# A two-block layer stack on one core: eleven small edits to the written order of VectorE, ScalarE, GpSimd and TensorE

## What is computed

```python
def first_block(x, ...):
    for l in range(2):
        x = layer_norm(ALPHA * x + 0.5 * swiglu(x, ffn1_w13[l], ffn1_w2[l]), ...)
        x = layer_norm(ALPHA * x + mixer(x, w_in[l], ...), ...)      # hgrn2 recurrence + gated spatial unit
        x = layer_norm(ALPHA * x + 0.5 * swiglu(x, ffn2_w13[l], ffn2_w2[l]), ...)
def second_block(x, ...):
    for l in range(2):
        x = x + 0.5 * rms_norm(swiglu(rms_norm(x, g[0]), ...), g[1])
        x = x + rms_norm(token_mixer(rms_norm(x, g[2]), ...), g[3])  # dilated attention + two-way mLSTM
        x = x + 0.5 * rms_norm(swiglu(rms_norm(x, g[4]), ...), g[5])
```

## Time and profile before

| | before |
|---|---|
| device time, median of 3 | 2114.63 us |
| profiled execution: device time | 2114.63 us |
| profiled execution: span | 2112.9 us |
| TensorE matmul busy | 2090.4 us, 99% |
| VectorE busy | 1686.0 us, 80% |
| ScalarE busy | 1081.8 us, 51% |
| GpSimd busy | 84.5 us, 4% |
| mean rate of all DMA | 187 GB/s |
| granted TensorE clock | full in all 40 slices |

### The profile page before, as it was taken

How to read it: one execution, slowest core, us unless ns; L and a number is a source line. 1 busy time by engine, 2 the same in 40 slices (tenths; PEclk the granted TensorE clock), 3 DMA queues, 4 the chain that set the end, 5 groups by cost and what they waited for, 6 DMA issues and landing times.

```text
span 2112.9 us, 28855 instructions
## 1 busy us (share of the span) xinstructions
PE 2090.4 (99%) x10552; PEld 1774.3 (84%) x10552; DVE 1686.0 (80%) x3158; ACT 1081.8 (51%) x1568; POOL 84.5 (4%) x127
## 2 busy tenths in 40 slices
PE   8999999999999999999999999999999999999998
PEld 7887999888788799988878887988888888888886
DVE  6888766888888877778888887779888888678886
ACT  6445554544544455444454446575445445665543
POOL 0000010000000000000000001010000000101000
PEclk9999999999999999999999999999999999999999
DMA  7765755566566574656646666346665765645663
GB/s 249 234 194 169 224 166 157 188 217 191 174 218 196 174 234 139 190 168 224 196 153 213 215 191 196 125 136 207 214 195 171 220 196 163 185 140 165 214 191 98
DMA packets 314368, 395.56 MB, mean 187 GB/s; under 512 B 17972, under 2 KB 272212, under 8 KB 313972
## 3 DMA queue, kind: packets, MB, share of 16 engines
q1 hardware_dynamic: 309120, 375.52, 57.6%
q0 software_dynamic: 4944, 18.14, 2.7%
q10 hardware_dynamic: 164, 0.06, 0.0%
HBM read 392.59 MB, written 1.06 MB: 186 GB/s over the span
## 4 chain that ended last, share of the span: by engine, by line
PE 93%; DVE 4%; ACT 1%; issue 1%; DMA 1%; POOL 0%; SPq 0%; DVEq 0%; POOLq 0%; ACTq 0%
PE bank L309 25%; PE bank L311 25%; PE bank L310 25%; PE bank L303 4%; PE bank L304 4%; PE bank L305 4%; DVE w_lo L293 1%; PE bank L478 1%; DVE hidden L464 1%; PE bank L1442 1%; PE bank L1463 1%; PE bank L972 1%; DMA stage<-in_mix_w_in 1%; PE bank L1534 1%; ACT w_hi L286 0%
## 5 line engine op out<-in xcount | busy, mean ns | idle before, releaser
L286 ACT ACTIVATE w_hi<-stage 128x1024 fp32r<-128x1024 f32 x711 | 747.1, 1058 | 635.0 <-PE bank L311 527.2
L293 DVE TENSOR_TENSOR w_lo<-stage,w_hi 128x1024 fp32r<-128x1024 f32 x711 | 865.2, 1224 | 213.7 <-ACT w_hi L286 206.9
L309 PE MATMUL bank<-w_hi,xt_hi 128*128 128x512 f32 x1760 | 692.9, 394 | 0.6 <-DVE xt_lo L816 0.4
L311 PE MATMUL bank<-w_hi,xt_lo 128*128 128x512 f32 x1760 | 686.7, 390 | 0.0
L310 PE MATMUL bank<-w_lo,xt_hi 128*128 128x512 f32 x1760 | 686.5, 390 | 0.0
L464 DVE STREAM_TRANSPOSE hidden<-hidden 32x128 f32<-32x128 f32 (+1 forms) x1376 | 391.7, 285 | 21.3
L309 PEld LDWEIGHTS bank<-w_hi,xt_hi 128*128 128x128 f32 x1760 | 331.0, 188 | 69.6 <-issue 1.2
L311 PEld LDWEIGHTS bank<-w_hi,xt_lo 128*128 128x128 f32 x1760 | 330.9, 188 | 68.8
L310 PEld LDWEIGHTS bank<-w_lo,xt_hi 128*128 128x128 f32 x1760 | 331.1, 188 | 66.5
L309 PE MATMUL bank<-w_hi,mt_hi 128*128 128x512 f32 x768 | 304.1, 396 | 6.7 <-DVE mt_lo L546 6.7
L311 PE MATMUL bank<-w_hi,mt_lo 128*128 128x512 f32 x768 | 299.8, 390 | 0.0
(11 more groups left out here) (275 smaller groups left out, 1384.2 us busy)
## 6 DMA issues: line engine op xcount, KB each, us to landing
stage<-in_ffn_w SPq DMA_DIRECT2D x352, 256.0 KB, 3.2
stage<-in_ffn_w_in SPq DMA_DIRECT2D x352, 256.0 KB, 3.2
stage<-in_ffn_w SPq DMA_DIRECT2D x88, 512.0 KB, 3.7
stage<-in_ffn_w_out SPq DMA_DIRECT2D x88, 512.0 KB, 3.7
stage<-in_w_in SPq DMA_DIRECT2D x80, 512.0 KB, 4.1
stage<-in_mix_w_in SPq DMA_DIRECT2D x56, 512.0 KB, 3.9
stage<-in_w_out SPq DMA_DIRECT2D x16, 512.0 KB, 4.1
stage<-in_mix_w_out SPq DMA_DIRECT2D x16, 512.0 KB, 3.4
```

Of the source, the lines that this page charges most:

```text
L286: act.activation(w_hi[:, u % RING, :], stage[:, u % STAGED, :], ACT.Copy).then_inc(S["hi_ready"], 1)
L293: dve.tensor_tensor(w_lo[:, u % RING, :], stage[:, u % STAGED, :], f32(w_hi[:, u % RING, :]), ALU.subtract).then_inc(S["lo_ready"], 1)
L309: pe.matmul(o, m_hi, hi, start=first, stop=False)
L311: return pe.matmul(o, m_lo, hi, start=False, stop=last)
```

## The change

- VectorE and TensorE, ffn stages from s = 2 on: the product (t = 1, i = 0) is transposed by TensorE, no longer by VectorE. The sixteen VectorE transposes of (0, 1), until now eight each at units 8 and 9, all stand at unit 7. Block transposes stand behind the multiplications of their unit (which moves something in stage 0 alone, besides this).
- VectorE, end of every ffn stage: `dve_norm_var` of tile 0 stands ahead of the multiplication of (1, 10).
- mix1: one more `w_lo` (unit 24) ahead of line 1156; GpSimd's broadcast loads no longer wait for ScalarE's sigmoid.
- mix2: `gate_bounds` moves from head 1 to head 0; `conv_in(3)` moves behind the `w_lo` of head 4; at the end ScalarE makes all `w_hi` up to unit 40 ahead of the squares of tile 0; VectorE makes the `w_lo` of unit 38 between the variance and x.
- GpSimd, ffn stages: `load_rows` no longer waits for unit 30's `w_hi`; it comes as soon as the stage before is done with its rows.

```diff
         def pe_turns(s):
-            return [(0, 0)] + ([(1, 0), (0, 1), (1, 1)] if s == 0 else []) + [(0, STEPS - 1), (1, STEPS - 1)]
+            return [(0, 0), (1, 0)] + ([(0, 1), (1, 1)] if s == 0 else []) + [(0, STEPS - 1), (1, STEPS - 1)]
         def turned_count(s, t, i):
-            return ffn_no(s) * 3 + (3 if s else 0) + pe_turns(s).index((t, i)) + 1
+            return ffn_no(s) * 4 + (2 if s else 0) + pe_turns(s).index((t, i)) + 1
...
-            first = [(8, 2, 10, [(0, 1)]), (10, 2, 12, [(1, 0)])] if s else [(16, 2, 18, [(0, 2)])]
+            first = [(7, 1, 9, [(0, 1)])] if s else [(16, 2, 18, [(0, 2)])]
...
             dve_norm_start(dve, s, 0)
+            dve_norm_var(dve, s, 0)
             dve_gate(dve, s, 1, STEPS - 1)
-            dve_norm_var(dve, s, 0)
             dve_norm_x(dve, s, 0)
...
-            lo_upto(dve, base + 24)
+            lo_upto(dve, base + 25)
             dve.wait_ge(S["hg_q"], at("hg_q", L, 1))
...
             pool_hold(pool, S["x_ready"], x_done(s - 1, 1))
-            pool_hold(pool, S["hg_sig"], at("hg_sig", L))
...
             merged_hi(3)
-            hi_upto(act, b + 38)
+            hi_upto(act, b + 40)
+            hi_upto(act, b + 41)
             act_norm_sq(act, s, 0)
-            hi_upto(act, b + 40)
             act_xt(act, s + 1, 0)
-            hi_upto(act, b + 41)
             act_pre_sq(act, s + 1, 0)
...
-
-            def gate_bounds():
-                rev = (slice(None), slice(None, None, -1))
                 for d in range(2):
                     dve.wait_ge(S["g_scan"], at("g_scan", L, 2))
...
                 if h == 4:
                     conv_in(2)
-                    conv_in(3)
                 lo_upto(dve, base + units_by_head(h) + RING)
...
                 if h == 1:
                     conv_in(0)
-                    gate_bounds()
...
                 if h == 4:
+                    conv_in(3)
                     conv_taps(1, (3, 4))
...
             dve_norm_var(dve, s, 0)
+            lo_upto(dve, base + 39)
             dve_norm_x(dve, s, 0)
...
-                    pool_hold(pool, S["hi_ready"], FIRST[s] + 3 * RING)
                     load_rows(pool, s)
```

More of the change, by code:

```diff
@@ L639, in dve_ffn @@
                             dve_h(dve, s, t, i)
[L640 to L643, removed]
                 for i in range(STEPS):
@@ L652, in dve_ffn @@
                         dve_h(dve, s, 1, i)
+                for v0, length, _, tiles in block_turns(s):
+                    if v0 <= v < v0 + length:
+                        for a in range(4 * (v - v0) // length, 4 * (v - v0 + 1) // length):
+                            dve_turn_blocks(dve, s, tiles, a)
             dve_norm_start(dve, s, 0)
+            dve_norm_var(dve, s, 0)
             dve_gate(dve, s, 1, STEPS - 1)
-            dve_norm_var(dve, s, 0)
             dve_norm_x(dve, s, 0)
```

## The result

| | before | changed |
|---|---|---|
| device time, median (4 runs each) | 2115.05 us | 2128.1 us (2126.98 to 2129.0) |
| ratio of the runs, 95% interval | | 1.006 (1.0045 to 1.0076) |
| profiled execution: device time, span | 2114.63, 2112.9 us | 2128.41, 2126.7 us |
| TensorE matmul busy | 2090.4 us | 2098.2 us |
| VectorE busy | 1686.0 us | 1662.4 us |

Slower, by 13 us, as forecast in direction. The forecast was 2122.0 us with a range up to 2126.0, so the size is outside it. Matmul busy time grew by 7.8 us, where the forecast had 1.6, and the mean granted clock of TensorE fell.

What follows compares the result with a forecast made beforehand. TensorE's matmuls, busy 2090.4 of a 2112.9 us span, were taken as the bound. Terms 1.6 - 2.4 - 4.2 + 3.0 + 9.1 + 0.3 = +7.4 gave 2122.0 us, range 2115.0 to 2126.0.

Steps and rivals of the forecast that it cites:

- the variance: Ends of ffn stages: x starts earlier, gaining 0.61 in each of four stages and 1.05 in four others; -2.4 and -4.2.
- The transposed product: Seven ffn stages: two more 128x128 instructions on TensorE cost 0.227 us each stage, +1.6; bounds nothing to +3.2.
- The middle of mix2: Moved `gate_bounds` and `conv_in(3)` make ScalarE and the convolution's input late; 1.5 per mix2, +3.0 in all.
- The waiting at the end of mix2: Line 478: squares behind unit 40's load make TensorE wait 4.1 us; with 0.4 behind it 4.5 per mix2, +9.1.
- The first part of the profile reading: Whole kernel: TensorE busy 2090.4 of 2112.9 us at full clock, no clock to win, 22.5 us removable without fewer matmuls.
- the burst: Sixteen block transposes at unit 7 delay unit 11's `w_lo`; slack 1.1, so nothing; up to 0.5 in three stages if slipping.
- the rows: Gain rows loaded in the ffn stages' first units; copies have slack to TensorE, +0.3 in all, bounds 0 and +3.
- rival D: Row loads hold the weights in six ffn stages, up to 1.0 each; +5.7, 2127.7 us; chance 0.12.
- mix1: The extra `w_lo` ahead of line 1156 falls into VectorE's idle time, and TensorE has no stall before; 0.
- B: Not slower: squares at the end of mix2 don't wait for unit 40's load; 2112.9 or 2109.4 us; chance 0.12.
- C: Smaller mix2 costs, +0.8 in the middle and +6.0 at the end; +2.1, 2116.7 us; chance 0.16.

Runs made afterwards that it cites:

- experiment 2: The changed kernel with the unit 41 copy moved behind the squares of tile 0 at the end of mix2; 2122.99 us.
- experiments 6: The changed kernel with the ffn stages' gain rows again held until unit 30's `w_hi`; 2126.28 us.
- experiment 7: The changed kernel with the sixteen block transposes of (0, 1) again split over units 8 and 9; 2125.81 us.
- experiment 1: The changed kernel with ScalarE's order at the end of mix2 put back as before; 2116.88 us.
- experiment 3: The changed kernel without the `w_lo` of unit 38 between variance and x at the end of mix2; 2127.13 us.
- experiment 4: The kernel before with only ScalarE's `w_hi` up to unit 40 put ahead of the squares at the end of mix2; 2124.52 us against 2116.44.

## Why the prediction was off

**Right:** the variance. Its two sizes, 0.61 and 1.05, measured 0.59 and 1.07, and its part alone was shown. The transposed product, 0.227 forecast and 0.25 measured per stage. Here a reading was wrong and the size right: the matmul that the prediction calls the next one after the pair (line 310, at 564.04 in the earlier trace rows) is the second. One of line 309 stands between, as the changed kernel shows at the same place:

```profile
563.64 0.38 PE L443 MATMUL bank<-const,hidden 128*128 128x128 f32 x2
563.78 0.48 PE L309 MATMUL bank<-w_hi,xt_hi 128*128 128x512 f32 x1
564.09 0.39 PE L310 MATMUL bank<-w_lo,xt_hi 128*128 128x512 f32 x1
```

So the 0.45 us hold the pair and one matmul, and less one matmul (0.23) they still give 0.22; but 0.45 was no bound for the pair. One of the two lasts 0.27 us, which is not what it takes from the stream.

The middle of mix2, 1.5 and 1.63. The waiting at the end of mix2, 4.1 (the terms add up to 4.0) and 3.95 to 4.11, with the hold of GpSimd beside the `w_lo`.

**Failed, the largest part of it:** "TensorE's order is unchanged, so it waits 4.1 us there; the late low parts of the next stage's x and the chain of tile 1 behind it add 0.4." I priced a stall of 4 us at its own length. The first part of the profile reading set the clock aside ("at the full granted clock, so no clock is to be won"); that nothing was to be won did not mean that nothing could be lost. No stall in the steady part of the kernel before was longer than 1.0 us, so its trace could not show the slow stretch there. Beyond the idle time stage 7 lost 2.1 us and stage 10 lost 1.2, against the 0.4 of that step; experiment 2 puts 1.9 of the 2.1 down to the clock. Forecast +9.1, measured +11.4.

**Failed, smaller:** "Slack 1.1, so nothing" for the burst and "Copies have slack to TensorE there, so +0.3 in all" for the rows. Each slack was real, shown by experiments 6 and 7, but both steps spent the same one. The forecast of rival D (rows hold the weights) was a loss in six stages of up to 1.0; it came in one stage, of 1.9, where a third row is loaded. The prediction called stage 6 the tightest for the burst; with the rows early it was stage 5, then 3 and 2. (The waits of the earlier trace rows are from the start of stage 8, not 9.) The same in mix1: two edits that cost nothing each alone cost 0.4 us together in the kernel before and 1.0 in the changed one.

**The end of the sum:** 7.4 forecast; 2.3 more at the mix2 ends, 1.6 in stage 5, 1.0 in mix1, 0.3 in the middle, 0.1 for the transposed product, 0.85 of the start and 0.3 of small steps make 13.8. No single one of these leads out of the range by itself.

**The rivals:** B (not slower) fell with experiment 1: the squares do wait for unit 40's load. C asked for lower costs in mix2, and they were higher. D had its mechanism in one place out of six; that its 2127.7 us lies next to the measured 2128.1 is luck, since rows and burst together made 1.9 of the 13.8 us.

## What to carry to other kernels

A stall of the matmul engine is not priced at its length alone: where it is longer than any that the profile shows, look at what the granted clock does behind it, and add the slow stretch as a term with bounds (here some 1 to 2 us behind stalls of 2.6 to 4.2). When several edits each use a slack, write the slack down once and subtract them one from another; two edits that cost nothing alone cost 1.9 us together here. Moving a reduction's last step ahead of an unrelated multiplication was worth 6.7 us, and being short it can be tried alone first.

## What the runs showed of the hardware

In the steady part of the kernels, TensorE's waits at line 478 show this. Behind idle times of 1.07 and 2.56 us the granted clock stayed full. Behind ten others it was down: 2.59, 2.61, 2.80, 3.17, 3.35, 3.63, 3.83, 3.95, 4.11 and 4.22 us (0.50 to 0.73 in the lowest 4 us slice of the view at each place, eight transposes taking 1.41 to 1.97 us, for 1.03 without a wait). 2.56 and 2.61 in one and the same kernel went different ways, so the length of the idle time alone doesn't decide here. Nor need the clock be down when the work begins again: in stage 7 of experiment 3 the transposes began at 1424.21, and the granted clock was 1.00 until 1424.7 and 0.50 from 1424.8.

Beyond the idle time a stage lost 0.9 to 1.4 us in the eight places where the clock was down for the shorter time, and 2.1 and 2.3 in the two where it was down about twice as long (stage 7 of the changed kernel, stage 10 of experiment 7). The slow stretch need not cost what it is long: in stage 7 of experiment 4, where the clock stayed full, a later wait of 0.9 us brought the loss to the same 4.0 us as in stage 10.
